# A hybrid encoder trunk on one core: the first layer's third fill copied ahead of a split, its loads reordered, and expert 0's places by two products

## What is computed

```python
for layer in range(DEPTH):
    hn = rmsnorm(h, mix_norm_pre[layer])
    proj = jnp.einsum('bsd,de->bse', hn, w_in[layer])   # u, q, k, v: 512 columns each
    y_pool = pool_mixer(u, pool_w[layer], pool_scale[layer])
    y_na = neighbourhood_attention(q, k, v, na_rpb[layer])   # 16 heads of 32, 4 x 64 grid, window of columns, bias
    mix = jnp.einsum('bse,ed->bsd', jnp.concatenate([y_pool, y_na], axis=-1), w_out[layer])
    h = h + rmsnorm(mix, mix_norm_post[layer])
    hn = rmsnorm(h, ffn_norm_pre[layer])
    if layer % 2 == 0:
        f = swiglu(hn, dense_w_gate[j], dense_w_up[j], dense_w_down[j])      # 4096 wide
    else:
        f = moe_swiglu(hn, moe_router[j], moe_w_gate[j], moe_w_up[j], moe_w_down[j])  # 2 of 8 experts, 3584 wide
    h = h + rmsnorm(f, ffn_norm_post[layer])
```

## Time and profile before

| | |
|---|---|
| three timed runs, us | 1308.52, 1310.09, 1312.76 |
| profiled execution, us | 1313.94 |
| its span, first to last instruction, us | 1312.1 |
| TensorE busy | 1287.3 us, 98% |
| VectorE, ACT, GpSimd busy | 31%, 22%, 8% |
| moved by DMA | 443.5 MB, 338 GB/s over the span |
| mean granted TensorE clock | 0.992 |

### The profile page before, as it was taken

One profiled execution on the slowest core, in us unless ns is written; L12 is line 12 of the kernel. 1 busy time (PEld: TensorE's weight loads), 2 busy tenths in 40 slices (PEclk: granted clock), 3 DMA queues, 4 the chain that ended last, 5 costly groups with the idle time before them and its releaser, 6 DMA issues.

```text
span 1312.1 us, 31069 instructions
## 1 busy us (share of the span) xinstructions
PE 1287.3 (98%) x14401; PEld 795.7 (61%) x14401; DVE 404.4 (31%) x565; ACT 286.7 (22%) x433; POOL 107.7 (8%) x240
## 2 busy tenths in 40 slices
PE   8999999999999999999999999999999999999996
PEld 8888999999989863354353364345353355336443
DVE  6777545555576750030110130030030031031011
ACT  4665444444465630000000000000000000000101
POOL 4133400000000307300000000000000000000000
PEclk9899999999999989999999999999999999999999
DMA  9537855555544399999999999999999999999994
GB/s 306 216 134 223 266 192 193 194 193 193 189 146 175 125 425 427 427 421 394 429 424 425 425 425 426 426 425 425 425 424 425 427 425 424 425 426 425 426 424 178
DMA packets 66868, 443.50 MB, mean 338 GB/s; under 512 B 4504, under 2 KB 10656, under 8 KB 42160
## 3 DMA queue, kind: packets, MB, share of 16 engines
q1 hardware_dynamic: 64592, 433.58, 81.3%
q0 software_dynamic: 2144, 7.90, 2.1%
HBM read 439.36 MB, written 2.10 MB: 336 GB/s over the span
## 4 chain that ended last, share of the span: by engine, by line
PE 91%; DMA 4%; DVE 2%; SPq 1%; ACT 1%; issue 0%; ACTq 0%; DVEq 0%
PE psum L1072 38%; PE psum L1081 18%; PE psum L726 9%; PE psum L728 9%; PE psum L727 9%; DMA unit<-in_moe_w_down 3%; PE psum L1016 2%; PE psum L1027 1%; PE psum L823 1%; PE psum L814 1%; DMA ring<-in_w_in 1%; SPq L384 1%; PE psum L840 1%; ACT pt L1225 1%; PE psum L755 1%; DVE hs L1520 0%
## 5 line engine op out<-in xcount | busy, mean ns | idle before, releaser
L1072 PE MATMUL psum<-unit,xT 128*32 128x448 f32 x5376 | 507.0, 539 | 0.1
L1072 PEld LDWEIGHTS psum<-unit,xT 128*32 128x32 f32 x5376 | 174.3, 110 | 327.5 <-issue 325.4
L1081 PE MATMUL psum<-unit,hid 128*32 128x256 f32 x4704 | 259.1, 379 | 3.2 <-DMA unit<-in_moe_w_down 3.2
L1081 PEld LDWEIGHTS psum<-unit,hid 128*32 128x32 f32 x4704 | 151.4, 110 | 108.4 <-issue 5.3
L1739 DVE TENSOR_TENSOR hidp<-hid,psum 128x448 f32<-128x448 f32 x42 | 38.5, 917 | 535.4 <-PE psum L1072 535.4
L726 PE MATMUL psum<-hT_hi,w_hi 128*128 128x256 f32 x656 | 184.0, 280 | 0.9 <-DVE w_lo L1419 0.8
L1419 DVE TENSOR_TENSOR w_lo<-ring,w_hi 128x2048 fp32r<-128x2048 f32 x64 | 148.0, 2321 | 116.6 <-ACT w_hi L1184 116.3
L728 PE MATMUL psum<-hT_hi,w_lo 128*128 128x256 f32 x656 | 182.7, 279 | 0.0
L727 PE MATMUL psum<-hT_lo,w_hi 128*128 128x256 f32 x656 | 182.7, 278 | 0.0
L1184 ACT ACTIVATE w_hi<-ring 128x2048 fp32r<-128x2048 f32 x71 | 135.3, 1911 | 65.1 <-PE psum L728 52.8
L726 PEld LDWEIGHTS psum<-hT_hi,w_hi 128*128 128x128 f32 x656 | 124.2, 189 | 3.1 <-issue 2.5
(11 more groups left out here) (253 smaller groups left out, 944.8 us busy)
## 6 DMA issues: line engine op xcount, KB each, us to landing
unit<-in_moe_w_gate SPq DMA_DIRECT2D x64, 1792.0 KB, 32.6
unit<-in_moe_w_up SPq DMA_DIRECT2D x64, 1792.0 KB, 27.2
unit<-in_moe_w_down SPq DMA_DIRECT2D x64, 1792.0 KB, 32.0
ring<-in_dense_w_gate SPq DMA_DIRECT2D x8, 2048.0 KB, 9.0
ring<-in_dense_w_up SPq DMA_DIRECT2D x8, 2048.0 KB, 9.0
ring<-in_dense_w_down SPq DMA_DIRECT2D x8, 2048.0 KB, 8.3
ring<-in_w_in SPq DMA_DIRECT2D x6, 2048.0 KB, 8.7
ring<-in_w_out SPq DMA_DIRECT2D x4, 2048.0 KB, 7.7
```

What stands on the lines that cost most here:

```text
L1072: ins = mm(bank(half, s)[quad(j)], xT[:, s, dt, :], w[:, at:at + FJ], start=dt == 0, stop=dt == DT - 1)
L1081: ins = mm(down_out[s][quad(j)], e[:, half, s, t, :], w, start=half == t == 0 and s != 2, stop=half == 1 and t == FT - 1, skip_group_check ...
```

## The change

Four edits. The identity is loaded by itself into its part of `cst`, with a semaphore of its own that the first transposes wait for; the rest of `cst` comes behind block 0. Of the bias words, quarter 0 is issued before the second half of block 1, quarter 1 behind it, quarters 2 and 3 behind block 2. In layer 0 ACT copies fill 2 ahead of the splits of halves 3 and 4; layer 1 keeps the old order. In the routing one product with the triangular matrix serves both columns, and the all-one product is added to the second; there were three products before. TensorE waits for the rest of `cst` ahead of the loop over the groups.

```diff
-            sp.dma_start(cst[:, :], consts).then_inc(cst_landed, 16)
+            sp.dma_start(ident, consts[:, K_ID:K_ID + P]).then_inc(ident_landed, 16)
...
                 if seq == 1:
-                    for quarter in range(2):
-                        load_rwords(sp, 0, quarter)
+                    load_rwords(sp, 0, 0)
                 sp.dma_start(dst, src).then_inc(w_landed[seq % RING], 16)
+                if seq == 0:
+                    sp.dma_start(cst[:, P:K_ALL], consts[:, P:K_ALL]).then_inc(cst_landed, 16)
                 if seq == 1:
-                    for quarter in range(2, 4):
-                        load_rwords(sp, 0, quarter)
+                    load_rwords(sp, 0, 1)
+                if seq == 2:
+                    load_rwords(sp, 0, 2)
+                    load_rwords(sp, 0, 3)
...
                 pe.wait_ge(cols_ready, 1)
+                pe.wait_ge(cst_landed, 16)
...
-                mm(pa[:, C4:C4 + 1], tri, sel0[:, 0:1], start=True, stop=True)
-                mm(pa[:, C4 + 1:C4 + 2], ones, sel0[:, 0:1], start=True, stop=False)
-                mm(pa[:, C4 + 1:C4 + 2], tri, sel0[:, 1:2], start=False, stop=True).then_inc(count0_done, 1)
+                mm(pa[:, C4:C4 + 2], tri, sel0, start=True, stop=False, skip_group_check=True)
+                mm(pa[:, C4 + 1:C4 + 2], ones, sel0[:, 0:1], start=False, stop=True, skip_group_check=True).then_inc(
+                    count0_done, 1)
...
-            pe.wait_ge(cst_landed, 16)
+            pe.wait_ge(ident_landed, 16)
...
                 split_to(h0 + 3)
                 act.preload_act_table(ACT.Exp)
                 fill_q()
+                if layer == 0:
+                    fill(2, kT[:, 0:2, :])
                 split_to(h0 + 5)
-                fill(2, kT[:, 0:2, :])
+                if layer:
+                    fill(2, kT[:, 0:2, :])
                 split_to(h0 + 6)
```

More of the change, by code:

```diff
@@ L279, in hybrid_encoder @@
         cst_landed = sem("cst_landed")
+        ident_landed = sem("ident_landed")
         x_landed = sem("x_landed")
```

## The result

The changed kernel took 1314.13 us in the median of seven runs (1312.85 to 1316.21), the kernel before 1310.58 (1308.52 to 1312.76). The ratio is 1.0029, with a 95% interval of 1.0017 to 1.0040: +3.55 us in the medians, +2.2 to +5.2 by the interval. The forecast was +0.8 us, 1310.9, with a range that ended at 1314.0. The lowest of the changed kernel's seven times lies above the highest of the other seven, by 0.09 us. In the profiled executions the spans are 1314.4 against 1312.1 us. The profiled execution of the changed kernel, 1316.21 us, is the slowest of its seven, 2.1 above their median.

A forecast was written before the change was run, and what follows sets the result against it. The weight stream was taken to set the end from the expert stage on, with everything ahead one chain passing shifts through. Copy +0.8, loads 0, routing 0, added to the median of 1310.09, gave 1310.9 us; range 1307.0 to 1314.0.

The forecast's parts named there:

- the early copy holds up half 3: First mixing stage: ACT's copy waits for the third fill, delaying half 3's split; TensorE idles 5.25 us in one piece.
- The idle term: TensorE before the second scores: one 5.25 us hole replaces 0.84 and 2.31 us; by idle time alone costs 2.1 us.
- The recipe for the work behind the hole: Fourth fill to second scores: 6.2 us at full clock, plus 2.1 lost to slow clock, plus 0.2 correction.
- The cover in the loop: Loop behind the second scores: 1.7 us of 4.1 remain before TensorE's turning, so no new wait; shift passes on.
- The loads at zero: SyncE's new load order: third load lands about 31.0 instead of 33.69, worth zero with the early copy in place.
- the term "before": Kernel before, second scores at 43.00: the whole 6.83 us slow clock stretch taken as lying over work.
- the routing's 0.42 us arrives: Rival in the routing stage: the shorter chain reaches the end, forecast less 0.42 us, 1310.5; chance 0.08.
- the lowest case: Clock stays up behind the hole before the fourth fill, leaving only idle time: -1.7 us, 1308.4; chance 0.15.
- the highest case: TensorE resumes the fourth fill at 36.4, slow stretch wholly over work, second scores at 46.2: +3.2 us, 1313.3.
- the additions on the split: Rival: a GpSimd addition delays half 3's `w_lo` by up to 1.45 us; slow stretch over work, +3.2 us; chance 0.17.
- the clock doesn't fall in the changed kernel: Rival at the hole before the fourth fill: only idle time counts, -1.7 us, 1308.4; chance 0.15.
- the early copy pays as meant: Rival on ACT: half 3's split precedes the copy, saving the wait and most slow work, -5.6 us, 1304.5; chance 0.05.

The follow-up runs named there:

- the second trace: Changed kernel run once more unchanged for its trace: hole 4.90 us, slow work 3.4 us, second scores at 43.08; 1312.95 us.
- the three traces: Three profiled executions of the changed kernel, nothing further changed: 1316.21, 1312.95 and 1313.70 us.
- four traces: Four profiled executions of the kernel before, nothing changed: 1313.94, 1309.43, 1311.32 and 1312.01 us.
- the second trace of before: Kernel before run once more unchanged for its trace: holes 0.8 and 2.33 us, no slow work, second scores at 39.84; 1309.43 us.
- the fourth trace: Kernel before run unchanged for a fourth trace: holes 0.9 and 2.32 us, no slow work, second scores at 40.17; 1312.01 us.

## Why the prediction was wrong

**Right, by its steps.** The idea that the early copy holds up half 3: copy at 30.1 (measured 30.01 in the second trace, 31.11 in the first, which had begun 1 us later), split behind it, TensorE back at 34.95 to 36.4 (34.88, 35.00, and 36.64 with the late start), one hole of 4.8 to 6.3 us (4.90, 4.90, 5.56). The idle term of +2.1 us: the means of the holes are 5.12 and 2.88, +2.2. The third load near 31 us and of no use there (issued at 17.80, 13.6 us to landing). The recipe for the work behind the hole, too: for the second trace it gives 34.88 + 6.2 + 1.7 + 0.2 = 42.98, the row says 43.08. The cover in the loop held: behind the hole there is no further wait of TensorE in the first mixing stage of the changed kernel. The loads at zero in the presence of the early copy: copy alone 1.0021, whole change 1.0029, with overlapping intervals. And the shift passed on: between the first traces it is 2.52 us at the second scores and 2.78 at the first expert unit (443.29 against 440.51).

**Right in part by luck: the slow work after.** The forecast put the fall at 32.7 and 4.15 us of slow work behind the hole; the three traces have 4.91, 3.41 and 4.53, mean 4.3. But only the third fell at 32.70. The first fell at 34.73, and the second at 35.08, behind the hole, where a stretch of 6.83 us as assumed would have cost 3.4; it was half as long.

**Wrong: the term "before".** The step that failed is "in the kernel before, the whole 6.83 us lay over work". True of the trace, and false of the executions whose median the difference was then added to. Over four traces the slow work averages 2.6 us (0, 0, 3.4 and 6.8), which costs 1.3, not the 3.4 that the sum let the change give back. With 1.3 in its place, the forecast's own numbers give: idle +2.1, clock 2.1 less 1.3 = +0.8, together +2.9 us. The means of the traces say +3.1, the timed runs +3.55 (+2.2 to +5.2). The rest lies within that interval; four traces are few, and their mean cost of 1.3 is known to about a microsecond at best. No rival of the prediction had a kernel *before* whose clock stays up, though it had one for the kernel after. The base moved as well: the forecast added to the median of three, 1310.09, and that of the seven runs is 1310.58.

**Wrong: the reading of the gap to the median.** The prediction noted that the profiled execution took 3.85 us more than the median, and added its difference to the median all the same. Against the second trace of before, 4.51 us faster, the first lost 3.16 us by the second scores, and 4.06 by the first expert matmul, where the routing's longer slow stretch comes in. A slow stretch that is in the one trace and not in the typical run must not be taken out of the typical run's time. The gap by itself proves no stretch, though: the fourth trace, without one, also took 1312.01.

**Wrong: the range's upper end.** The lower end takes the lowest case, -1.7, and 1.6 of scatter from it; the upper end is the highest case, +3.2 us or 1313.3, rounded, without the 2.7 of scatter that the same sentence names. With it the range would have ended at 1316.0. There is a slip in the recipe too: twice its own 0.74 and 2.73 us from 36.23 is 43.2, not 42.8 (a matmul in the slow stretch takes 0.213 us where the recipe's 0.1135 doubled is 0.227), so its correction of +0.2 is worth up to 0.4 us less.

**Wrong, though the sum didn't hang on it: what sets the end.** The prediction let the weight stream set the end and the routing's delays vanish under it. In fourteen traces a late unit is issued 742.56 to 742.63 us after the first expert matmul, whatever the first unit's time, so the units follow TensorE as it frees their places, and 1.2 us lost in the routing arrive in full. The rival that the routing's 0.42 us arrives has these traces for it; no timed run is fine enough to show it.

**Wrong: the chances.** "Slower by over 0.3%" was put at 0.12 with +0.8 as the centre; measured is 0.29% with an interval of 0.17 to 0.40%, at the edge of that case. From the corrected centre of +2.9 it deserved more. Of the rivals, the additions on the split did happen in the first trace (`w_lo` of half 3 took 2.96 us, 0.67 more than undisturbed) and were nearly absent in the second; alone they explain little. That the clock doesn't fall in the changed kernel, another rival, happened in none of its three traces. The rival that the early copy pays as meant fell: ACT's order is what the trace shows.

The Trainium skill ("TensorE: Matmul & The Clock Gate", Part 1) says that the activity window of the clock runs free and doesn't reset when the kernel starts, so that the place of a transition varies. The traces agree that the place varies, and show more: holes of 2.0 to 2.3 us of the same cause were followed by a slow stretch of 6.8 us at once, by one of 3.4 us that began 1.5 us later, and twice by none.

## What to carry to other kernels

A copy that waits for an engine must not stand ahead of work whose data is already there and for which the same engine will ask next: look for the place in the in-order queue where neither holds up the other, here one split later. Before a difference is taken from one trace and added to a median, compare that trace's own time with the median; if they stand apart by about the price of a slow clock stretch that the trace shows, suspect that the stretch is not in the typical execution, and take more traces of the same kernel: here it was in two of four. Give a range's upper end the same scatter as its lower one. In this kernel a hole of 2.0 to 2.4 us brought the slow clock in two of five traces, an idle one of 4.9 to 5.6 us in four of four.

## What the runs showed of the chip that was not expected

The opening 28 matmuls took from 7.75 to 9.37 us over the traces, so the first transposes began between 9.13 and 10.39 us: a scatter of about 1 us before any data is used. The kernel before absorbs this in its holes, the changed one does not. Behind holes of 2.0 to 2.3 us of the same cause the work lost 0, 1.7 or 3.4 us to the clock, and the routing had a slow stretch of either length in every trace of before (clock 0.66 or 0.83 over 480 to 490 us). VectorE subtractions with both inputs in SBUF took about 1 us longer beside GpSimd additions (3.12 instead of 2.29, 2.29 instead of 1.22), and so did the scaling of probabilities by a factor per row (2.06 instead of 0.94), enough to turn into a wait of 1.0 to 1.3 us of TensorE as soon as its earlier holes were gone.
